# Reordering the mixer of an attention and RWKV/mLSTM network, and its first norms, on one core

## The chip, the cores and the metric

The kernel runs as one program on 1 core of one Trainium2 chip. The metric is the device time of one execution in microseconds. The core has five engines with instruction streams of their own: TensorE (PE, with weight loads as PEld), VectorE (DVE), ScalarE (ACT), GpSimd (POOL) and SyncE (SP, which here only issues DMAs). Each stream runs in order; semaphores tie them together.

## What the reference computes

Everything is float32, 256 tokens of width 1024. Two networks run one after the other.

The first has two layers over `x` (256 tokens) and a context `ctx` (256 tokens). In each layer both are normed and modulated, projected, and go through windowed attention and a Fourier mix, an output projection and a SwiGLU. The shifts and gains of the modulation come from `silu(c) @ w_ada`, a product of 1024 by 6144 for each layer (the "ada" chunks):

```
h  = rmsnorm(x,   g) * (1 + sc1)  + sh1
hc = rmsnorm(ctx, g) * (1 + csc1) + csh1
p = h @ w_in ; kv = hc @ w_in[:, kv]          # 10 column tiles of 128
```

The second has two layers: SwiGLU, mixer, SwiGLU. The mixer projects the normed tokens to 47 column tiles (r, k, v, low-rank inputs, mq, mk, mo, mv, gates) and runs two recurrences in chunks of 64 tokens. RWKV-7 needs for each head and chunk five masked 64x64 products of the scaled r, k, kk and b, and an inverse. mLSTM needs a causal convolution of mq and mk with four taps, a scan over its forget gates, and scores weighted by exponentials:

```
out = conv_b + sum_j w[j] * z[t - 3 + j]       # mq and mk, then silu
kk = k*k_k / ||k*k_k|| ; a = sigmoid(..) ; decay = exp(-exp(w_log))
S = S*w - (S kk) b^T + v k^T ;  y = S r        # done in chunks of 64
```

## The kernel before, in words

All features lie on partitions, tokens along the free axis. Weights come in chunks of 1 MB (two tiles of 128 columns) through `ring_a`, two slots; SP issues a load when the chunk before it in that slot has been used (`load_a`, line 478). In the second network each product is made of three products of rounded parts (`split_product`, lines 1645 to 1647): ACT rounds a weight tile to `t_hi` (`round_t`, L817), and DVE (tiles 0 to 16 of the mixer) or POOL (from tile 17, `rest_t`, L554) forms the rest `t_lo`. `t_hi` and `t_lo` hold two tiles, so tile t+2 is rounded only when tile t has been multiplied.

**The start.** Eight ada chunks come first: two in `ring_a`, six loaded ahead into `work` (L493). `ada` multiplies a chunk (L1592), ACT copies the row (L744), `ada_turn` turns it (L1603), DVE adds the bias (L1011). The norms of `x` and `ctx` follow ada chunks 5 and 6: squares on ACT (L596), their sums (L1615), two small products (L1624, L1633), then DVE scales by gain and norm (L1040) and ACT adds the shift (L767). Two more ada chunks (`B0`) stand between the norms and the first projection (L1717), which waits for all of it. Layer 0's attention takes 9 ada chunks in each of its two calls, one for each step over pairs of heads.

**The middle of the mixer**, in each of its two layers. TensorE's order: tiles 0 to 17, three low-rank products, tiles 18 to 26 (in layer 1 the value-residual product after tile 23), sums of squares for the head norms (L1964), their spread over the channels (L1972), the bonus sums (L1977), value tiles 27 and 28 (`value_tiles`, L1919), transposes of v (L1984), the two gate rows (L1994, L1995), transposes of khc and bhc, value tiles 29 and 30, and the unit products at, a, mrt, mt, art (`per_unit`, L2018). Then comes the front of the mLSTM heads (from L2062), which waits for DVE's last mask, for the silu of the convolution and for the gate rows.

DVE's order: shifts of tiles 0 to 14, the norm and decay chain (L1292 to L1340), the scaled operands kt, bh, kh, rt, khc, bhc (L1344 to L1352), all four taps of the convolution (L1362 and L1365, 32 instructions), the gate rows (L1374 to L1389), the masks of the unit products (L1393, L1410 to L1416). ACT empties tiles in order, between sigmoids, exponentials, the moves of the transposed tiles (L904) and the silu (L925).

Of the kernel before, what the change touches and what calls it, by code (L numbers as in the profile page):

```python
# [23 lines left out]
ALU = mybir.AluOpType  # L24
# [3 lines left out]
P = 128  # L28
# [27 lines left out]
ADA_STEP0, ADA_STEP1 = 9, 12  # L56
# [115 lines left out]
def program(nc, wa, wd, c1_in, c2_in, vec_in, small_in, four_in, x_in, ctx_in, out):  # L172
    with ExitStack() as ctx:
# [85 lines left out]
        def const1(name):  # L259
# [43 lines left out]
        in_loaded, vec_loaded, c2_loaded, const_loaded, small_loaded, out_stored = (  # L303
            sem(n) for n in ("in_loaded", "vec_loaded", "c2_loaded", "const_loaded", "small_loaded", "out_stored"))
# [30 lines left out]
                    "kt", "bh", "kh", "rt", "khc", "bhc", "at", "x1", "xt1", "x", "xt", "mrt", "mt", "art",  # L335
                    "s1", "ym", "yc", "yq", "s2", "yr", "yn", "gn", "gb", "ya"])
        RA = Steps(["tanh", "sgx", "sw", "aa", "gg", "rsq", "e0", "e1", "e2", "vt", "khct", "bhct", "ysd", "yT"])
        RP = Steps(["lw", "la", "lg", "ss", "rnb", "bon", "vt", "khct", "bhct", "at", "a", "mrt", "mt", "art", "yT"])
# [8 lines left out]
        MVS = Steps(["c0", "c1", "c2", "c3", "mn", "lf", "F", "g", "M", "fm", "nm", "hc"]  # L347
# [33 lines left out]
        ada_parts = [("0", ADA_FIRST - ADA_EARLY), ("early", ADA_EARLY), ("B0", ADA_FILL), ("L0", 2 * ADA_STEP0), ("M00", ADA_FILL), ("M01", ADA_FILL),  # L381
# [50 lines left out]
        def fill(name):  # L432
            return range(ada_from[name], ada_from[name] + ADA_FILL)
# [135 lines left out]
        def _(act):  # L569
            act.dma_start(vec[:, :], vec_in).then_inc(vec_loaded, 16)  # L570
            act.dma_start(c2[:, :], c2_in).then_inc(c2_loaded, 16)
            act.dma_start(x[:, :, :], x_in).then_inc(in_loaded, 16)
            act.dma_start(xc, ctx_in).then_inc(in_loaded, 16)
# [5 lines left out]
            def norm(key, src, call=None, ready=None, onto=None, first=None, also=None, summed=None):  # L579
# [26 lines left out]
                act.wait_ge(norm_sum, n + 1)  # L606
                nc.scalar.copy(nrt[:, :], ps[:, norm_bank(key), 0:T]).then_inc(norm_part, 1)
                act.wait_ge(norm_tok, n + 1)
# [138 lines left out]
            for g in range(ADA_FIRST):  # L747
                ada(g)
                if g == ADA_FIRST - 4:
                    act.wait_ge(in_loaded, 32)  # L750
                    act.wait_ge(c2_loaded, 16)
                    norm(("pre_mix", 0, 0), x[:, :, :])
                if g == ADA_FIRST - 3:
                    norm(("pre_mix", 0, 1), xc)
            act.dma_start(c1, c1_in).then_inc(const_loaded, 16)
            act.dma_start(wfour.rearrange("p a b -> p (a b)"), four_in).then_inc(const_loaded, 16)
            fcall = acall = 0
            for l in range(LAYERS):
# [4 lines left out]
                for which in range(2):  # L763
                    for k in range(KD):
                        act.wait_ge(norm_scaled, n_two[("pre_mix", l, which)] * KD + k + 1)
                        to = h2[:, k, token_cols(l, which)]
                        ins = nc.scalar.activation(to, to, ACT.Identity, bias=shift_of(l, 0, which)(k))  # L767
                    ins.then_inc(norm_out, 1)
                for g in fill(f"B{l}"):
                    ada(g)  # L770
                stage, n_q, n_blk = f"proj1{l}", (2 * T, T)[l], (4, 2)[l]
# [32 lines left out]
            for l in range(LAYERS):  # L804
# [31 lines left out]

                def empty_values(t):

                    act.wait_ge(t_done, l * NT2 + t + 2)
                    both = ps[:, 5 if t == MV else 7, :].rearrange("p (b s n) -> p s b n", b=2, s=2)  # L840
# [20 lines left out]
                empty_t(15)  # L861
# [5 lines left out]
                empty_t(16)  # L867
# [10 lines left out]
                empty_t(17)  # L878
                act.wait_ge(rw_p, RP.at("lg", l))
                nc.scalar.copy(gg, ps[:, 6:8, :].rearrange("p a (b t) -> p (a b) t", t=T)).then_inc(rw_a, 1)  # L880
                for t in range(18, 24):
                    empty_t(t)
# [6 lines left out]
                for t in range(24, MV):  # L889
                    empty_t(t)  # L890
# [1404 lines left out]
```

## Time and profile before

| | us |
|---|---|
| median of 3 runs | 2630.38 (2629.23 to 2631.09) |
| the profiled execution | 2632.37 |
| its span | 2630.5 |
| busy in the span: PE / PEld / DVE / ACT / POOL | 2446.0 / 2212.9 / 1257.7 / 995.0 / 220.3 |

The span runs from the first instruction to the last; 1.87 us of the execution lie around it. PE is busy for 93% of the span. That PE is busy does not say that it runs at full clock: the granted clock, 1.00 being 2.4 GHz and 0.50 being 1.2 GHz, is a column of its own where a table of stretches is shown.

### The profile page before, as it was taken

The numbers are of one execution on the slowest core, as the hardware profiler recorded it, in microseconds if no ns is written. First come the engines' busy times: TensorE is split into PE (matmuls) and PEld (weight loads), VectorE is DVE, ScalarE is ACT, GpSimd is POOL, SyncE is SP. The second block draws the span as 40 slices with busy tenths as digits, with TensorE's granted clock in tenths as the row PEclk, the third lists the DMA queues.
The fourth block names the chain that finished last, engine by engine and source line by source line (L and its number), as shares of the span: only waits on it lengthen the run. The fifth ranks groups of instructions, "written<-read, shape, count | busy, mean of one in ns | idle before, by whom it ended". The sixth has DMA issues, their size and how long they took to land.

```text
span 2630.5 us, 50338 instructions
## 1 busy us (share of the span) xinstructions
PE 2446.0 (93%) x20748; PEld 2212.9 (84%) x20748; DVE 1257.7 (48%) x2006; ACT 995.0 (38%) x1579; POOL 220.3 (8%) x199
## 2 busy tenths in 40 slices
PE   6989799989989889989999898999999997989998
PEld 3755499879966689989998788899999996888998
DVE  1043165455523255555564753455555548443554
ACT  2054343353333353343345332334434354321433
POOL 0000000000000000010004231100100032321000
PEclk9999899989989989999999799999999998999999
DMA  6144355345413455434433122554444341114552
GB/s 270 65 156 165 112 192 191 112 184 191 175 73 144 177 193 183 175 140 184 183 109 140 41 74 82 211 185 175 168 176 183 112 155 54 66 66 160 196 187 96
DMA packets 64487, 388.06 MB, mean 148 GB/s; under 512 B 7152, under 2 KB 7280, under 8 KB 27376
## 3 DMA queue, kind: packets, MB, share of 16 engines
q1 hardware_dynamic: 63216, 379.61, 39.6%
q10 hardware_dynamic: 864, 5.16, 0.5%
q8 instruction: 90, 1.47, 0.2%
q0 software_dynamic: 288, 1.57, 0.2%
q14 instruction: 29, 0.24, 0.0%
HBM read 385.27 MB, written 1.05 MB: 147 GB/s over the span
## 4 chain that ended last, share of the span: by engine, by line
PE 81%; DVE 9%; ACT 4%; DMA 3%; issue 2%; POOL 2%; SPq 0%; DVEq 0%; POOLq 0%; ACTq 0%
PE ps L1645 19%; PE ps L1646 19%; PE ps L1647 19%; PE ps L1717 5%; PE ps L1730 2%; PE ps L2150 2%; DMA ring_a<-in_wa 2%; PE ps L2018 2%; PE ps L2188 2%; POOL h_lo L532 1%; PE ps L1615 1%; PE ps L2123 1%; DVE nsq L1365 1%; PE ps L1592 1%; DVE work L1143 1%
## 5 line engine op out<-in xcount | busy, mean ns | idle before, releaser
L1645 PE MATMUL ps<-h_hi,w_hi 128*128 128x256 f32 x2464 | 701.9, 285 | 12.4 <-DVE mod L1011 8.7
L1646 PE MATMUL ps<-h_lo,w_hi 128*128 128x256 f32 x2464 | 699.9, 284 | 0.0
L1647 PE MATMUL ps<-h_hi,w_lo 128*128 128x256 f32 x2464 | 699.7, 284 | 0.0
L1645 PEld LDWEIGHTS ps<-h_hi,w_hi 128*128 128x128 f32 x2464 | 475.8, 193 | 14.6 <-DVE mod L1011 9.6
L1646 PEld LDWEIGHTS ps<-h_lo,w_hi 128*128 128x128 f32 x2464 | 475.9, 193 | 0.1
L1647 PEld LDWEIGHTS ps<-h_hi,w_lo 128*128 128x128 f32 x2464 | 475.7, 193 | 0.0
L1070 DVE TENSOR_TENSOR w_lo<-ring_a,w_hi 128x1024 fp32r<-128x1024 f32 x308 | 366.5, 1231 | 30.3 <-ACT w_hi L621 30.1
L1645 PE MATMUL ps<-hid_hi,d_hi 128*128 128x256 f32 x1232 | 348.7, 283 | 0.0
L1646 PE MATMUL ps<-hid_lo,d_hi 128*128 128x256 f32 x1232 | 348.7, 283 | 0.0
L1647 PE MATMUL ps<-hid_hi,d_lo 128*128 128x256 f32 x1232 | 348.6, 283 | 0.0
L621 ACT CAST w_hi<-ring_a 128x1024 fp32r<-128x1024 f32 x308 | 306.0, 1044 | 62.0 <-DMA ring_a<-in_wa 62.0
L1104 DVE TENSOR_TENSOR hid<-sg,ps 128x256 f32<-128x256 f32 x154 | 64.9, 421 | 550.9 <-ACT sg L652 550.8
L652 ACT ACTIVATE sg<-ps 128x256 f32<-128x256 f32 x154 | 59.1, 384 | 684.8 <-PE ps L1647 684.8
L1645 PEld LDWEIGHTS ps<-hid_hi,d_hi 128*128 128x128 f32 x1232 | 236.5, 192 | 0.0
L1646 PEld LDWEIGHTS ps<-hid_lo,d_hi 128*128 128x128 f32 x1232 | 236.5, 192 | 0.0
L1647 PEld LDWEIGHTS ps<-hid_hi,d_lo 128*128 128x128 f32 x1232 | 236.5, 192 | 0.0
L1645 PE MATMUL ps<-h_hi,t_hi 128*128 128x256 f32 x688 | 203.1, 295 | 7.9 <-POOL h_lo L532 3.8
L1077 DVE TENSOR_TENSOR d_lo<-ring_d,d_hi 128x1024 fp32r<-128x1024 f32 x154 | 190.3, 1236 | 19.7 <-ACT d_hi L629 16.7
L629 ACT CAST d_hi<-ring_d 128x1024 fp32r<-128x1024 f32 x154 | 161.6, 1049 | 98.3 <-PE ps L1647 98.3
L532 POOL TENSOR_TENSOR h_lo<-nsq,h_hi 128x256 fp32r<-128x256 f32 x72 | 60.8, 869 | 1647.0 <-ACT h_hi L640 922.0
L1646 PE MATMUL ps<-h_lo,t_hi 128*128 128x256 f32 x688 | 197.0, 286 | 0.0
L1647 PE MATMUL ps<-h_hi,t_lo 128*128 128x256 f32 x688 | 196.6, 286 | 0.0
(275 smaller groups left out, 3304.1 us busy)
## 6 DMA issues: line engine op xcount, KB each, us to landing
ring_a<-in_wa SPq DMA_DIRECT2D x278, 1024.0 KB, 4.8
ring_d<-in_wd SPq DMA_DIRECT2D x154, 512.0 KB, 5.3
work<-in_wa SPq DMA_DIRECT2D x6, 1024.0 KB, 22.0
work<-in_small POOLq DMA_DIRECT2D x2, 768.0 KB, 5.7
c<-in_c ACTq DMA_DIRECT2D x1, 1175.0 KB, 10.8
work<-in_c ACTq DMA_DIRECT2D x1, 1088.0 KB, 4.9
x<-in_x ACTq DMA_DIRECT2D x1, 1024.0 KB, 15.2
work<-in_ctx ACTq DMA_DIRECT2D x1, 1024.0 KB, 19.6
```

What stands on the lines that cost most here:

```text
L532: nc.gpsimd.tensor_tensor(h_lo[:, k, :], nsq[:, k, :], h_hi[:, k, :].bitcast(F32), ALU.subtract)\
L621: nc.scalar.copy(w_hi[:, f % 2, part], ring_a[:, c % 2, part]).then_inc(hi_a, 1)
L629: nc.scalar.copy(d_hi[:, f % 2], ring_d[:, d % 2]).then_inc(hi_d, 1)
L652: nc.scalar.activation(sg[:, f % 2, :], ps[:, 4 + f % 2, 0:T], ACT.Silu).then_inc(sg_ready, 1)
L1070: ins = nc.vector.tensor_tensor(w_lo[:, f % 2, part], ring_a[:, c % 2, part], w_hi[:, f % 2, part].bitcast(F32), ALU.subtract)
L1077: nc.vector.tensor_tensor(d_lo[:, f % 2], ring_d[:, d % 2], d_hi[:, f % 2].bitcast(F32), ALU.subtract)\
L1104: nc.vector.tensor_tensor(hid[:, f % 2, :], sg[:, f % 2, :], ps[:, 4 + f % 2, T:2 * T], ALU.mult)\
L1645: nc.tensor.matmul(out, hi, to_hi, start=start, stop=False, skip_group_check=True)
L1646: nc.tensor.matmul(out, hi, to_lo, start=False, stop=False, skip_group_check=True)
L1647: return nc.tensor.matmul(out, lo, to_hi, start=False, stop=stop, skip_group_check=True)
L1717: mm = nc.tensor.matmul(ps[:, 4 + p % 2, 0:cols.stop - cols.start], ring_a[:, slot, i % 2, k, :], h[:, k, cols], start=(k == 0), stop=(k = ...
L1730: mm = nc.tensor.matmul(ps[:, 4 + p % 2, b * P:(b + 1) * P], h[:, k, b * P:(b + 1) * P], ring_a[:, slot, i % 2, k, :], start=(k == 0), sto ...
```

## The change

Start: the norm of `x` and that of `ctx` are spread between ada chunks 3 to 7. For layer 0, `x` is scaled by its norm alone, before the gain is known, and ACT applies gain and shift together (`shifted`), alternating between `x` and `ctx` for each of the 8 channel tiles. The first projection tile waits for one channel tile of `ctx` at a time (`h2_part`) and no longer for the whole norm. `B0` is gone; its two chunks go to layer 0's attention, whose step 4 takes two chunks in each call. The DMAs of the constants are issued after the 16 shifts. In layer 1 ACT now copies the two B1 rows ahead of the 16 shifts, and DVE adds their bias halfway in the second norm.

Mixer: the head-norm sums stand behind tile 18, the spread and the bonus behind tile 21, then tile 22, the transposes of v, tile 23, products at and a, tile 24, transposes of khc, product mrt, tile 25, products art and mt, tile 26, transposes of bhc, value tiles 27 and 28, the gate rows, value tiles 29 and 30. DVE masks each product in between; the convolution follows the last mask. ACT writes the first tap of the convolution while it empties tiles 15 to 22 (`empty_conv`).

```diff
-("B0", ADA_FILL)
+("B0", 0)
-each = [1 if l == 0 or n % 4 else 2 for n in range(PAIRS + 1)]
+each = [2 if n % 4 == 0 and (l or n == 4) else 1 for n in range(PAIRS + 1)]
...
+            def shifted(which, k):
+                act.wait_ge(norm_scaled, n_two[("pre_mix", l, which)] * KD + k + 1)
+                gains = gain_of(l, 0, which)(k) if (l, which) == (0, 0) else 1.0
+                return nc.scalar.activation(to, to, ACT.Identity, scale=gains, bias=shift_of(l, 0, which)(k))
...
+            def empty_conv(t):
+                act.wait_ge(t_done, l * NT2 + t + 1)
+                k, src = t - MQ, ps[:, 4 + t % 2, 0:T]
+                nc.scalar.activation(z[:, t, 1:T + 1], src, ACT.Copy)
+                nc.scalar.activation(nsq[:, k, :], src, ACT.Identity, scale=vcol(f"tap3{l}", k),
+                                     bias=vcol(f"conv_b{l}", k)).then_inc(t_free, 1)
+                round_t(t + 2)
...
+                    if mixed is not None and k < KD - 1:
+                        pe.wait_ge(h2_part, mixed * (KD - 1) + k + 1)
...
             # TensorE, the mixer behind the low-rank products
+                tile(18)
                 # layer 1: value-residual product; head-norm sums (L1964 before)
+                for t in range(19, 22):
+                    tile(t)
                 # spread (L1972), bonus (L1977)
+                tile(22)
+                pe.wait_ge(rw_a, RA.at("gg", l))
+                to_tokens(z[:, V0:V0 + QT, 1:T + 1], 6).then_inc(rw_p, 1)
+                tile(23)
+                pe.wait_ge(rw_v, RV.at("bh", l))
+                per_unit(0, bh, kt).then_inc(rw_p, 1)
+                per_unit(2, kt, bh).then_inc(rw_p, 1)
+                tile(24)
+                pe.wait_ge(rw_v, RV.at("khc", l))
+                pe.wait_ge(rw_a, RA.at("vt", l))
+                to_tokens(khc, 6).then_inc(rw_p, 1)
+                pe.wait_ge(rw_v, RV.at("at", l))
+                per_unit(0, kh, rt).then_inc(rw_p, 1)
+                tile(25)
+                pe.wait_ge(rw_v, RV.at("x1", l))
+                per_unit(2, bh, rt).then_inc(rw_p, 1)
+                pe.wait_ge(rw_a, RA.at("khct", l))
+                per_unit(6, kh, kt).then_inc(rw_p, 1)
+                tile(26)
+                pe.wait_ge(rw_v, RV.at("mrt", l))
+                to_tokens(bhc, 0).then_inc(rw_p, 1)
+                value_tiles(MV)
+                pe.wait_ge(rw_v, RV.at("art", l))
                 # gate rows (L1994, L1995)
+                value_tiles(MV + 2)
```

## Rows read from the trace of the kernel before

**Rows 1.** The page: the chain that ended last, shares by engine.

```profile
PE 81%; DVE 9%; ACT 4%; DMA 3%; issue 2%; POOL 2%; SPq 0%; DVEq 0%; POOLq 0%; ACTq 0%
```

**Rows 2.** Chain of waits in the first 90 us: start, duration, what.

```profile
21.64 1.93 PE ps L1592 x16
...
46.69 0.19 DVE gain L1022
...
53.67 5.35 DMA ring_a<-in_wa
...
59.15 31.14 PE ps L1717 x67
```

**Rows 3.** Stretches: length, busy (instructions) by engine, granted clock, DMA share, GB/s.

```profile
21.64:51.60 29.96, 23.30 (x156) 13.57 (x160) 4.70 (x17) 11.94 (x28) 0.00 (x0) 1.00 0.62 252
1407.57:1434.77 27.20, 26.97 (x217) 26.16 (x216) 7.76 (x10) 11.57 (x17) 21.59 (x17) 1.00 0.44 155
1440.73:1448.00 7.27, 7.27 (x17) 5.34 (x17) 3.47 (x3) 2.95 (x3) 0.00 (x0) 0.50 0.00 0
1461.45:1468.92 7.47, 7.47 (x50) 7.34 (x52) 7.40 (x21) 5.25 (x9) 0.00 (x0) 0.77 0.21 89
1468.85:1474.66 5.81, 5.81 (x193) 5.68 (x192) 5.78 (x9) 3.82 (x5) 4.03 (x3) 1.00 0.03 6
1489.50:1503.90 14.40, 14.40 (x43) 11.85 (x44) 2.23 (x4) 2.13 (x4) 0.00 (x0) 0.50 0.00 0
```

**Rows 4.** Timeline of ACT, first products: start, busy, line, what, idle before.

```profile
47.41 3.30 ACT L767 ACTIVATE work<-work,mod 128x256 f32<-128x256 f32 x8 [2.32 <-DVE work L1040]
68.44 0.37 ACT L775 COPY work<-ps 128x256 f32<-128x256 f32 x1 [12.47 <-PE ps L1717]
```

**Rows 5.** Timeline of PE, three steps of layer 1's attention.

```profile
840.86 1.13 PE L1771 MATMUL ps<-work 64*128 64x512 f32 x4 [0.20 <-ACT work L700]
...
846.37 1.13 PE L1771 MATMUL ps<-work 64*128 64x512 f32 x4 [0.52 <-ACT work L700]
...
853.79 1.13 PE L1771 MATMUL ps<-work 64*128 64x512 f32 x4
```

**Rows 6.** Layer 1's first projection: chain of waits.

```profile
759.13 4.91 DMA ring_a<-in_wa
```

**Rows 7.** Timeline of PE: spread, transposes, value tiles and front, both mixers.

```profile
1440.73 3.77 PE L1972 MATMUL ps<-work,c 8*128 8x256 f32 x8 [4.06 <-DVE work L1332]
...
1456.34 1.97 PE L1984 MATMUL ps<-c,work 128*128 128x128 f32 x16
...
1461.45 0.35 PE L1919 MATMUL ps<-t_hi,h_hi 128*128 128x256 f32 x1 [3.15 <-POOL t_lo L554]
...
1489.50 3.75 PE L2062 MATMUL ps<-work,c 4*128 4x256 f32 x8 [4.70 <-DVE work L1393]
...
2182.25 3.77 PE L1972 MATMUL ps<-work,c 8*128 8x256 f32 x8 [5.84 <-DVE work L1332]
...
2230.96 3.75 PE L2062 MATMUL ps<-work,c 4*128 4x256 f32 x8 [5.26 <-DVE work L1393]
```

**Rows 8.** Timeline of DVE in both mixers.

```profile
1437.91 0.98 DVE L1330 TENSOR_SCALAR work<-work 8x256 f32<-8x256 f32 x1 [22.52 <-ACT work L892]
...
1440.60 1.15 DVE L1334 TENSOR_TENSOR work<-work 128x1024 f32<-128x1024 f32 x1
...
2166.20 1.49 DVE L1308 TENSOR_TENSOR work<-vfirst,work 128x1024 f32<-128x1024 f32 x1 [22.62 <-ACT work L886]
...
2170.34 5.02 DVE L1318 TENSOR_SCALAR work<-work,vec,omka 128x256 f32<-128x256 f32 x4
```

**Rows 9.** Timeline of POOL between the value tiles, mixer layer 0.

```profile
1456.20 5.10 POOL L554 TENSOR_TENSOR t_lo<-ring_a,t_hi 128x512 fp32r<-128x512 f32 x4 [17.45 <-ACT t_hi L817]
```

**Rows 10.** Timeline of ACT between the value tiles and the front.

```profile
1455.07 2.00 ACT L817 CAST t_hi<-ring_a 128x1024 fp32r<-128x1024 f32 x2
...
1476.66 1.91 ACT L925 ACTIVATE nsq<-nsq 128x2048 f32<-128x2048 f32 x1 [3.87 <-DVE nsq L1365]
```

More of the change, by code:

```diff
@@ L55 @@
 ADA_FILL = 2
-ADA_STEP0, ADA_STEP1 = 9, 12
+ADA_STEP0, ADA_STEP1 = 10, 12
 PAIRS = 8
@@ L605, in norm, with norm_squares, norm_rows, norm_root @@
                     also()
-                act.wait_ge(norm_sum, n + 1)
+                norm_rows(key)
+                norm_root(key)
+            def norm_squares(src):
+                for i in range(PIECES):
+                    k = slice(i * KD // PIECES, (i + 1) * KD // PIECES)
+                    nc.scalar.activation(nsq[:, k, :], src[:, k, :], ACT.Square).then_inc(norm_sq, 1)
+            def norm_rows(key):
+                act.wait_ge(norm_sum, n_id[key] + 1)
                 nc.scalar.copy(nrt[:, :], ps[:, norm_bank(key), 0:T]).then_inc(norm_part, 1)
+            def norm_root(key):
+                n = n_id[key]
                 act.wait_ge(norm_tok, n + 1)
@@ L744, in ada @@
                 nc.scalar.copy(ada_rows[:, u, :], ps[:, 4 + u, 0:T]).then_inc(ada_row, 1)
[L747 to L756, printed above, removed]
+            first, second = ("pre_mix", 0, 0), ("pre_mix", 0, 1)
+            ada(0)
+            ada(1)
+            ada(2)
+            act.wait_ge(c2_loaded, 16)
+            act.wait_ge(x_loaded, 16)
+            nc.scalar.activation(warm[:, 0:1], const("one"), ACT.Sqrt)
+            norm_squares(x[:, :, :])
+            ada(3)
+            norm_rows(first)
+            act.wait_ge(xc_loaded, 16)
+            norm_squares(xc)
+            ada(4)
+            norm_root(first)
+            ada(5)
+            norm_rows(second)
+            ada(6)
+            norm_root(second)
+            ada(7)
             fcall = acall = 0
@@ L1026, in gains, with inverse, norm @@
                 dve.wait_ge(gain_ready, done)
-            def norm(key, src, gains, dst, shifted=False, onto=None, also=None):
+            def inverse(key):
+                dve.wait_ge(norm_rt, n_id[key] + 1)
+                nc.vector.reciprocal(nst[:, 2:4], nst[:, 0:2]).then_inc(norm_rstd, 1)
+            def norm(key, src, gains, dst, shifted=False, onto=None, halfway=None):
                 n = n_id[key]
@@ L1032, in norm @@
                     dve.wait_ge(norm_scaled, n_two[key] * KD)
-                dve.wait_ge(norm_rt, n + 1)
-                nc.vector.reciprocal(nst[:, 2:4], nst[:, 0:2]).then_inc(norm_rstd, 1)
-                if also is not None:
-                    also()
+                inverse(key)
                 dve.wait_ge(norm_all, n + 1)
@@ L1057, in norm @@
                 for k in range(KD):
+                    if k == KD // 2 and halfway is not None:
+                        halfway()
                     ins = scale(k)
@@ L1948, in _ @@
                 mm.then_inc(rw_p, 1)
-                for t in range(18, 24):
-                    tile(t)
+                tile(18)
                 if l:
@@ L1956, in _ @@
                     mm.then_inc(vres_p, 1)
-                for t in range(24, MV):
-                    tile(t)
                 pe.wait_ge(rw_v, RV.at("kq", l))
@@ L1966, in _ @@
                 mm.then_inc(rw_p, 1)
+                for t in range(19, 22):
+                    tile(t)
                 pe.wait_ge(rw_v, RV.at("rn", l))
```

239 lines of the change are left out of this document (125 added, 114 removed).

## The prediction

> **What bounds the kernel now.** I read the page's chain first. It lies on TensorE for 81% and on DVE for 9% [rows 1], so work of other engines matters only where TensorE stands still or runs slowly for it. Then I read the chain and the timelines where the change is. There are two kinds of such places.
>
> At the start the first projection begins at 59.15 although its inputs are nearly ready: its weights are asked for at 53.67, when the first B0 chunk has freed the slot, and take 5.35 us [rows 2]. Before that, from 21.64 to 51.60, TensorE is busy for 23.30 of 29.96 us [rows 3].
>
> In each mixer there are two stretches. First DVE stands for 22.52 us (layer 0) and 22.62 us (layer 1) and waits for ACT, which waits for products that TensorE issues behind its tiles [rows 8]. Then TensorE in turn waits for DVE, and the spread starts at 1440.73 and 2182.25 behind 4.06 and 5.84 us of idle time, the front at 1489.50 and 2230.96 behind 4.70 and 5.26 us [rows 7]. From spread to front it is 48.8 and 48.7 us. The clock falls there: 0.50 from 1440.73 to 1448.00 and 0.50 over the 14.4 us from the front on [rows 3], which is 1.2 GHz where the tiles ran at 2.4 GHz (1.00 from 1407.57 to 1434.77).
>
> **The start.** In the new order TensorE issues, from 21.64 on, the same kinds and numbers of instructions as it did up to 51.60: five ada chunks (3 to 7) with their turns, two sums, two pairs of token products, two spreads. Their busy time is 23.30 [rows 3], so with some 0.9 us of short waits it is through at 45.8. The last bias and the gain follow, as before at 46.69 [rows 2]; I take 46.4. Now `x` needs only ACT for each channel tile. ACT's 16 shifts take 3.30/8 = 0.41 each [rows 4], the second one waits one DVE scaling (about as long), so TensorE's first product can start at 47.4 and the last of the 8 channel tiles is there at 46.5 + 16 x 0.41 = 53.1. The weights are no wait any more: with B0 gone, SP asks for them as soon as ada chunks 0 and 1 are used, before 15 us, and those loads stand behind the early chunks exactly as the B0 loads did. Before, tile 0 took from 59.15 to 68.44, 9.3 us [rows 2, 4]. Now it ends between 54.0 (ACT bound) and 47.4 + 9.3 = 56.7 (as slow as it was). I take 55.0, since the idle time in front shrinks from 1.5 us behind other pauses to 1.6 us behind dense work: **-13.4 us** (-11.7 to -14.4). The constants' DMAs move from before the shifts to behind them, 0.8 us of issue on ACT while tile 0 runs; their first reader comes six tiles later, so nothing.
>
> **The two chunks that moved.** They go into step 4 of each attention call of layer 0. Layer 1 has such steps already: a step with one chunk lasts 846.37 - 840.86 = 5.5, one with two 853.79 - 846.37 = 7.4 [rows 5]. The lower price is 1.9; against the 5.1 us of an undisturbed step it would be 2.3. I take 2.3 for the first call and 2.7 for the second, whose steps are shorter while each chunk still needs about 5 us to land [rows 6]: **+5.0 us** (+3.8 to +7).
>
> **Layer 1's first norms.** ACT's 16 shifts now come behind the copies of both B1 rows, so they start near 760.7 and not at 755.4. The first product needs the 8 of `x` and one of `ctx`: 760.7 + 9 x 0.41 = 764.4. Before it waited for a load from 759.13 to 764.04 [rows 6], which the change leaves. **0** (-1 to +2).
>
> **The mixers, up to the spread.** One tile costs 27.20/9 = 3.02 [rows 3]. In layer 0 the head-norm sums (about 1.9, half of what the like spread took at the low clock [rows 7]) follow tile 18, and tiles 19 to 21 stand before the spread: 1407.6 + 2.9 + 1.9 + 3 x 3.02 = 1421.4 instead of 1440.73, so **-19.3**. DVE is ready by then: its chain ended at 1437.91 - 22.52 = 1415.4 [rows 8], the inverse root and its reciprocal need about 3 us more.
> In layer 1 (its times are layer 0's plus 737.1) the value-residual product also stands behind tile 18, and DVE's wait for it ends at about 1414.3 instead of 1429.1. From there to the spread DVE needed 2182.25 - 2166.20 = 16.0 [rows 7, 8], which gives 1430.3 instead of 1445.1, **-14.8**. TensorE then idles some 6 us before the spread, more than the 5.84 of before, so I give the spread and the bonus their old 7.5 us at 1.2 GHz, whereas in layer 0 they come behind dense tiles and take 3.8.
>
> **From spread to front.** At full clock, TensorE's order adds up to: spread and bonus 3.8, five tiles (22 to 26) 14.4, at 7.47 x 0.77 / 2 = 2.88 without waits, since a value pair is two tiles' work [rows 3], three sets of transposes at 1.0 (1.97 for two [rows 7]) 3.0, five unit products at 5.81/3 = 1.94 [rows 3] 9.7, and 1.1 for the wait on the second mask in layer 0: 32.0. Behind tile 26 the serial part begins, and it is the main cost of the change:
> - tile 28 can be rounded only when tile 26 is done and emptied: 0.4 + 1.04 on ACT, 2.5 to 3 on POOL (5.10/4 for each half [rows 9]), less the 1.0 of the transposes: 3.6;
> - value tiles 27 and 28: their like, 29 and 30, took 7.47 at a mean clock of 0.77 behind 3.15 us of idle time [rows 3, 7], and I take that;
> - tiles 29 and 30 can be rounded only now: emptying 0.65, one t_hi 1.0 [rows 10], four halves on POOL 5.1 [rows 9], together 6.9. Before, three sets of transposes and the gate rows stood in this gap and all but 3 us of it was used; now only the gate rows (1.0) do, and 5.9 is idle;
> - value tiles 29 and 30: 7.47;
> - ACT empties them 0.65, rounds two more tiles 2.0, loads a table 1.28 and makes the silu 1.91 [rows 10], which the front waits for: 6.1 with the gaps between. Before, DVE's convolution was later than this and hid it; now the convolution is through before value tiles 29 and 30.
> Sum 63.5 where it was 48.8. Layer 0: -19.3 + 14.7 = **-4.6**. Layer 1: no wait of 1.1, but 3.7 more for spread and bonus at the low clock, 66.1 against 48.7: -14.8 + 17.4 = **+2.6**. Together **-2.0**.
> The bounds: all value tiles at 2.4 GHz save 1.7 x 4 = 6.8; all of them wholly at 1.2 GHz (7.47 x 0.77 / 0.50 = 11.5 each) cost 16.1 more. The front itself ran at 0.50 for 14.4 us [rows 3]; the idle time in front of it grows from 4.7 to 6.1, so I leave it as it is.
>
> **What hides the rest.** The first tap on ACT adds 0.28 for each of 8 tiles, where ACT waits for TensorE anyway; it takes eight instructions off DVE. The masks read PSUM and lie between the tiles.
> DVE and POOL hinder each other: four scalings of 128x256 lasted 5.02 us in layer 1 [rows 8], where POOL was making t_lo, against 1.15 for a whole 128x1024 product without it. The 16.0 us that I use hold this already. The Trainium skill, "SBUF — State Buffer", section "Who interferes with whom", says that a VectorE instruction with two SBUF inputs and a GpSimd instruction that reads SBUF exclude each other for the whole instruction. That speaks against this change, since POOL's rests of tiles 22 to 28 now fall among DVE's unit work. It is my rival C.
> For the clock: the Trainium skill, "TensorE: Matmul & The Clock Gate", section "Why this matters for your kernels", says that idle gaps between bursts bring the array back to half its clock. By it the new gaps of 5.9 and 6.1 us cost what I have taken or more; without it rival A holds.
>
> **The sum.** -13.4 + 5.0 + 0 - 2.0 = -10.4. The profiled execution took 2632.37, its span 2630.5. From it the forecast is 2622.0; it lies 2.0 above the median of 2630.38, so for a median I say **2620.0**.
>
> **The rivals.**
> - A, the clock stays up. Value tiles at full clock (-6.8) and spread and bonus of layer 1 too (-3.7): 2620.0 - 10.5 = 2609.5. For it: more of TensorE's idle time is filled than before. Against it: value tiles behind only 3.15 us of idle time had 0.77. Chance 0.15.
> - B, the mixers give back more. Each value pair loses twice as much to the clock as the one in the rows, 1.7 x 4 = 6.9: 2626.9, no change that can be told. For it: the gaps of 5.9 us are longer than the 3.15. Against it: that pair was back at full clock before its end, since the unit products behind it had 1.00 [rows 3]. Chance 0.15.
> - C, the other side: POOL's halves queue behind DVE's long instructions. For tiles 22 to 28 each of two halves waits up to 1.15 for one, 2.3 a tile; seven tiles in two mixers make 32.2, if none of it has slack: 2652. For it: DVE works without pause from the spread to the last mask. Against it: a unit product or transposes stand between most tiles, 2 to 4 us of slack. Slower by 0.2% needs 15.6 us of it, about half. Chance 0.08.
> - D, the start gives less: should ACT's shifts and the pauses take the place of the load, with tile 0 ending at 60, it is 2625.0. Chance 0.07.
>
> **How the numbers follow.** The forecast has 0.55, with its own range of 2614 to 2626. 0.2% is 5.3 us, about what a measurement of this kernel can tell from no change: faster means below 2625.1, slower above 2635.6. Faster: A 0.15, most of the forecast 0.51, half of D 0.04, together 0.70. Slower: most of C and the tail of B, 0.09. Same: 0.21. The range leaves out the far half of C and of A: 2608 to 2632.
>
> **What would show it.** Right: the first projection at 47 to 48 and its tile 0 out by 57; two steps of layer 0's attention at about 7.4; the spreads some 19 and 15 us earlier against their mixer's start; 60 to 68 us from spread to front, with TensorE idle before both value pairs and before the front, the last one ended by ACT's silu. Wrong: DVE, not ACT, ending the wait at the front; TensorE waiting for t_lo before tiles 22 to 26 for more than 1 us each; a clock of 1.00 in the value tiles; a wait for weights at the first projection.

## The result, and the profile after

The changed kernel takes 2617.99 us (median of 5, 2613.37 to 2618.90); the kernel before, beside it, 2630.14 (5 runs, 2627.39 to 2631.09). The ratio is 0.9942, 95% interval 0.9932 to 0.9953. The forecast was 2620.0. The profiled execution took 2617.78, its span 2615.8: 14.7 us less than the span of before, which belonged to an execution 2.2 above its median.

The chain of the changed kernel by engine, against [rows 1]:

```profile
PE 79%; DVE 5%; issue 5%; POOL 4%; ACT 4%; DMA 2%; POOLq 0%; SPq 0%; DVEq 0%; ACTq 0%
```

TensorE has lost 2 points and DVE 4; POOL has gained 2 and issue (time in which an engine waited for nothing that the profile shows) 3.

**The start**, TensorE's timeline of the changed kernel (start, busy, line, what, idle before), against [rows 2, 3]. L1654 is an ada chunk, L1677 the sums, L1783 the projection:

```profile
24.11 1.93 PE L1677 MATMUL ps<-nsq,c 128*32 128x256 f32 x16
25.82 1.93 PE L1654 MATMUL ps<-work,cs 128*32 128x256 f32 x16
...
28.99 1.07 PE L1654 MATMUL ps<-work,cs 128*32 128x256 f32 x16
...
31.08 1.07 PE L1677 MATMUL ps<-nsq,c 128*32 128x256 f32 x16
...
36.41 0.51 PE L1665 MATMUL ps<-c,ada_rows 128*128 128x2 f32 x4
38.53 11.80 PE L1783 MATMUL ps<-work,ring_a 128*128 128x512 f32 x23 [1.62 <-ACT work L792]
```

From 28 on an ada chunk takes 1.07 us and not 1.93. The same instruction on the same data is 1.8 times as fast, so TensorE is at its higher clock there. In the profile of before all of them, up to 55, took 1.93 or close to it, while the column of the granted clock said 1.00 [rows 3]. In these profiles that column does not tell the speed at the start, before its first change; the duration of a known instruction does. Tile 0 leaves TensorE at 47.37, where it was 68.44. Its first products are slow again, in two stretches up to its end:

```profile
38.50:42.00 3.50, 3.47 (x5) 1.44 (x6) 2.08 (x6) 3.50 (x9) 0.00 (x0) 0.52 0.18 32
42.00:47.40 5.40, 5.40 (x14) 2.49 (x13) 0.00 (x0) 2.65 (x7) 0.00 (x0) 0.99 0.72 287
```

**Layer 0's attention**, the same timeline: a step of 5.1 us, then the one with two chunks, 7.43:

```profile
141.28 1.13 PE L1837 MATMUL ps<-work 64*128 64x512 f32 x4 [0.40 <-ACT work L713]
...
146.40 1.13 PE L1837 MATMUL ps<-work 64*128 64x512 f32 x4
...
153.83 1.13 PE L1837 MATMUL ps<-work 64*128 64x512 f32 x4
```

**The mixers**, TensorE's timeline of the changed kernel, against [rows 7]. L2040 is the spread, L1988 the value pairs, L2133 the front:

```profile
1404.90 0.36 PE L1707 MATMUL ps<-h_hi,t_hi 128*128 128x256 f32 x1 [1.25 <-POOL t_lo L555]
1407.94 1.99 PE L2040 MATMUL ps<-work,c 8*128 8x256 f32 x8
1442.57 0.55 PE L1988 MATMUL ps<-t_hi,h_hi 128*128 128x256 f32 x1 [3.37 <-POOL t_lo L555]
...
1457.87 0.55 PE L1988 MATMUL ps<-t_hi,h_hi 128*128 128x256 f32 x1 [5.81 <-POOL t_lo L555]
...
1471.55 3.75 PE L2133 MATMUL ps<-work,c 4*128 4x256 f32 x8 [5.89 <-ACT nsq L977]
...
2150.71 3.77 PE L2040 MATMUL ps<-work,c 8*128 8x256 f32 x8 [7.12 <-DVE work L1397]
```

Stretches of the changed kernel (columns as in [rows 3]): the two value pairs and the front of layer 0, then the two value pairs of layer 1:

```profile
1442.57:1451.10 8.53, 8.53 (x49) 8.40 (x50) 5.73 (x15) 0.00 (x0) 0.00 (x0) 0.66 0.00 0
1457.87:1465.66 7.79, 7.79 (x48) 7.59 (x48) 2.66 (x6) 0.00 (x0) 0.00 (x0) 0.73 0.22 93
1471.55:1485.95 14.40, 14.40 (x43) 11.85 (x44) 2.23 (x4) 3.34 (x5) 0.75 (x1) 0.50 0.15 64
2189.02:2196.52 7.50, 7.50 (x49) 7.37 (x50) 5.74 (x15) 0.00 (x0) 0.00 (x0) 0.77 0.01 2
2203.28:2210.51 7.23, 7.22 (x48) 7.02 (x48) 2.67 (x6) 0.00 (x0) 0.00 (x0) 0.80 0.23 95
```

**Where the time went, by stage.** DVE makes one small reciprocal for each norm. Its start marks the stages well, because the same instruction stands at the same place in every kernel. The table has these starts from the profiled execution of each run (us): the norm of `ctx` at the start, the norm behind layer 0's output projection, the last of layer 1's first norms; the lengths of the two mixers, from their norm to the norm behind them; and the last norm.

| kernel | ctx norm | out, layer 0 | layer 1 | mixer 0 | mixer 1 | last |
|---|---|---|---|---|---|---|
| before | 50.2 | 303.9 | 755.6 | 340.9 | 346.5 | 2622.0 |
| changed | 35.6 | 287.8 | 740.6 | 338.2 | 349.7 | 2607.3 |
| start_only | 35.2 | 286.3 | 740.7 | 341.3 | 346.3 | 2606.4 |
| mixer_only | 47.1 | 302.3 | 755.7 | 337.6 | 349.8 | 2621.2 |
| b0_only | 47.1 | 302.0 | 755.8 | 343.2 | 346.3 | 2624.6 |
| whole_norm | 39.6 | 297.3 | 750.6 | 340.2 | 350.1 | 2623.1 |
| silu_first | 35.8 | 288.2 | 742.5 | 331.9 | 343.7 | 2594.6 |
| gap_fill | 35.7 | 288.1 | 741.3 | 331.6 | 343.7 | 2593.8 |
| hi_first | 35.4 | 287.8 | 740.8 | 326.0 | 336.7 | 2583.1 |
| dve_rest | 39.5 | 288.8 | 742.6 | 326.4 | 342.8 | 2591.2 |
| early_root | 35.4 | 287.8 | 741.5 | 333.7 | 337.5 | 2590.3 |
| start_fill | 36.1 | 285.7 | 738.9 | 331.0 | 343.1 | 2591.2 |
| best | 39.6 | 292.5 | 745.6 | 320.6 | 328.4 | 2576.0 |
| wide_first | 39.9 | 297.2 | 750.6 | 319.0 | 326.9 | 2575.7 |

Changed against before: 15.0 us are won by layer 1's first norms, and the mixers add -2.7 and +3.2.

The same program differs between executions. The mixer of `before` and `b0_only` is the same code, 340.9 and 343.2. Single cells are good to about 2 us, and more at the start (below).

### The profile page after: what moved, and what is told of

The parts are those of the page before. It is cut to its first block, busy times and chain, and to the rows that moved or that the text cites. A ratio compares the mean times of both kernels' runs of the same rounds, so it can differ in the third digit from the quotient of the medians.

```text
span 2615.8 us, 50326 instructions
## 1 busy us (share of the span) xinstructions
PE 2434.9 (93%) x20748; PEld 2207.6 (84%) x20748; DVE 1248.7 (48%) x1990; ACT 1002.4 (38%) x1594; POOL 224.7 (9%) x199
## 4 chain that ended last, share of the span: by engine, by line
PE 79%; DVE 5%; issue 5%; POOL 4%; ACT 4%; DMA 2%; POOLq 0%; SPq 0%; DVEq 0%; ACTq 0%
PE ps L1707 19%; PE ps L1708 19%; PE ps L1709 19%; PE ps L1783 5%; POOL t_lo L555 3%; PE ps L1796 2%; PE ps L2221 2%; PE ps L2068 2%; DMA ring_a<-in_wa 2%; POOL h_lo L533 1%; PE ps L2259 1%; PE ps L1677 1%; PE ps L2194 1%; PE ps L1654 1%; PE ps L1811 1%
## 5 line engine op out<-in xcount | busy, mean ns | idle before, releaser
L1707 PEld LDWEIGHTS ps<-h_hi,w_hi 128*128 128x128 f32 x2464 | 476.6, 193 | 14.7 <-DVE mod L1063 9.6
## 6 DMA issues: line engine op xcount, KB each, us to landing
c<-in_c ACTq DMA_DIRECT2D x1, 1175.0 KB, 10.4
x<-in_x ACTq DMA_DIRECT2D x1, 1024.0 KB, 14.8
work<-in_ctx ACTq DMA_DIRECT2D x1, 1024.0 KB, 19.3
```

Source lines behind the costliest of these rows:

```text
L1707: nc.tensor.matmul(out, hi, to_hi, start=start, stop=False, skip_group_check=True)
```

## The experiments

### One part alone

`start_only` has the new start and first norms and the old mixers, `mixer_only` the reverse.

> The kernel before with the changed start, B0 chunks and layer 1 norms only; the mixers are the old ones. Theory 1 (the mixers cancel, -3.0 and +2.9 in the two profiles): all of the gain is here, 0.994 of the kernel before (2615 to 2619), first projection near 38.5 and its tile 0 out near 47.4, spread to front 48.8 as before. Rival (the new mixer has a hidden part in the gain, for instance through the 1.9 us that were lost between the attention and the second network): 0.996 to 0.997, 2620 to 2623.

> The kernel before with the new mixers only. Theory 1: within 0.1% of the kernel before (2630 +-2); layer 0 about 3 us shorter and layer 1 about 3 us longer, 63.6 and 65.7 us from spread to front. Rival: 4 us faster or more, 2626 or less.

Measured: `start_only` 2616.75 against 2632.73, ratio 0.9945 (0.9932 to 0.9959). `mixer_only` 2635.41, ratio 1.0010 (1.0001 to 1.0019), its mixers 3.3 us shorter and 3.3 longer. All of the gain is in the new start and first norms; the rivals of both are out. The new mixers as they stand are worth nothing, if not slightly less.

`b0_only` moves the two chunks and nothing else:

```diff
-("B0", ADA_FILL)
+("B0", 0)
-each = [1 if l == 0 or n % 4 else 2 for n in range(PAIRS + 1)]
+each = [2 if n % 4 == 0 and (l or n == 4) else 1 for n in range(PAIRS + 1)]
```

> The kernel before with only the two B0 chunks moved to step 4 of layer 0's two attention calls; the order of the norms stays. Theory 1: the weights of the first projection are there early, but the shifts of ctx end at 55.4, so the first product moves from 59.15 to 55.6 (-3.6); the two longer steps give back 4.2 to 5; the small products of the start stay at 1.93 us an ada chunk. Together +1, 2631, no change that can be told. Rival (the late load of the weights was most of the start's gain, and the order of the norms adds little): the start is 8 us or more shorter and the time 2626 or less.

Measured: 2634.90, ratio 1.0010 (1.0001 to 1.0019), as theory 1 had it. The first product came at 52.49 and not at 55.6, because this execution had its fast stretch early, as `mixer_only` had. TensorE's timeline of `mixer_only`, whose start is the old code:

```profile
41.19 1.07 PE L1601 MATMUL ps<-work,cs 128*32 128x256 f32 x16
...
55.73 2.68 PE L1726 MATMUL ps<-work,ring_a 128*128 128x512 f32 x3 [2.01 <-DMA ring_a<-in_wa]
```

The like rows of before are an ada chunk of 1.93 at 42.72 and the first product at 59.15. So the same code differs by 3.4 us between two executions. That difference does not last: 3.1 us at the norm of `ctx` (50.2 and 47.1) are 1.6 at the norm behind the output projection and nothing at the next norm (318.02 in before, 318.08 in `mixer_only`). Against `mixer_only` the moved chunks give 3.2 us at the start (55.73 to 52.49) and all but 0.3 of it is gone at the norm behind the output projection (302.3 and 302.0): the two longer steps cost 2.9 us.

### The wait by channel tiles

`whole_norm` is the changed kernel with the old wait at the first projections:

```diff
-                        project(stage, i, h2, slice(0, 2 * T), mixed=l)
+                        project(stage, i, h2, slice(0, 2 * T))
...
+                pe.wait_ge(norm_out, n_id[("pre_mix", l, 1)] + 1)
```

> The changed kernel, but its first projections wait for the whole norm of ctx, as before the change, and no longer for one channel tile at a time. Theory 1 (the wait by channel tiles is worth two things: it overlaps tile 0 with the shifts, and it leaves TensorE no 8 us of idle time that would halve its clock): the last shift ends at 44.6, the first product starts near 44.9 and tile 0 takes about 9.4 us at half clock, out near 54.5 where it was 47.37: 2618 + 7 = 2625. Rival (the clock does not depend on that pause): tile 0 takes 4.8 us and is out near 49.7: 2620.

Measured: 2631.09 (11 runs, 2624.81 to 2642.65), ratio 0.9999 (0.9987 to 1.0011): the whole gain is gone, 13 us by the medians where the expected time has 7. TensorE's and ACT's timelines:

```profile
33.53 1.94 PE L1677 MATMUL ps<-nsq,c 128*32 128x256 f32 x16
...
37.92 1.07 PE L1654 MATMUL ps<-work,cs 128*32 128x256 f32 x16
...
49.30 1.19 PE L1783 MATMUL ps<-work,ring_a 128*128 128x512 f32 x1 [7.79 <-issue]
```

```profile
58.67 0.37 ACT L815 COPY work<-ps 128x256 f32<-128x256 f32 x1 [9.47 <-PE ps L1783]
```

At its own place theory 1 holds: the first product has the double duration of 1.19 behind 7.8 us of idle time, and tile 0 takes 9.4 us. From the first shift to tile 0 it is 58.67 - 41.95 = 16.7 us against 47.37 - 37.36 = 10.0 in the changed kernel: 6.7 us for the wait. One thing was missing in it: in layer 1 the same wait costs 3.0: from its first norms (750.6 and 740.6 in the table) to the norm behind its output projection (910.4 and 897.4) it is 159.8 against 156.8 us. The shifts start 4.6 us later than in the changed kernel because the small products of this execution sped up at 37 and not at 28. The edit stands behind those products, and `dve_rest`, `best` and `wide_first`, which have no such edit, sped up as late in their profiles; so this belongs to the execution. The two waits make 9.7 us; why the medians differ by another 3.4 no run settles.

### The pauses in the mixer

`silu_first` is the changed kernel with two steps of ACT exchanged:

```diff
-                empty_values(MV + 2)
                 act.wait_ge(ml_v, MVS.at("c3", l))
                 nc.scalar.activation(nsq[:, :, :], nsq[:, :, :], ACT.Silu).then_inc(ml_a, 1)
+                empty_values(MV + 2)
```

> The changed kernel, ACT makes the convolution's silu before it empties value tiles 29 and 30 and rounds tiles 31 and 32, not behind them. Theory 1 (the 5.9 us of idle time in front of the front are ACT's order and nothing else): DVE's convolution is through at 1448, the silu ends near 1459.5, before the value tiles end at 1465.7; the front starts some 0.9 us behind them, 5 us earlier in each mixer: 2618 - 10 = 2608. If the clock then stays at 2.4 GHz over the front (14.4 us at 1.2 GHz now), up to 4 us more for each: 2600. Rival (DVE's gate rows or POOL's t_lo of tiles 31 and 32 are as late, the front's own tiles then wait for what the front no longer waits for): 2 us or less, 2616 to 2618.

Measured: 2608.47 against 2632.73, ratio 0.9917 (0.9903 to 0.9930), which is 6.6 us better than the changed kernel by the ratios. TensorE's timeline:

```profile
1466.11 1.96 PE L2133 MATMUL ps<-work,c 4*128 4x256 f32 x8 [0.83 <-ACT work L892]
```

The pause of 5.89 is 0.83, and the first products of the front take 1.96 and not 3.75. The mixers are 6.3 and 6.0 us shorter. The pause was ACT's order. By the medians the gain is 9.5 us; the profiled execution was the fastest of its five. The clock did not stay up: from 1468.8 to 1479.0 the granted clock is 0.52.

The next four start from `silu_first`. `hi_first` changes the order within a value pair (the comment stands for the loop's lines):

```diff
+                    pe.wait_ge(t_hi_ready, p0 + t + 2)
                     for b in range(2):
+                        # t_hi products of the block, then (b = 0: wait for t_lo) its t_lo products
```

> The last kernel (silu first), and in each value pair TensorE makes the 16 products of the first block of tokens with t_hi before it waits for t_lo; the other 32 follow. Theory 1 (what TensorE waits for ahead of the value pairs is POOL's t_lo, 3.37 and 5.81 us of idle time, and it is this idle time that brings the clock down in them): the pairs start when t_hi is rounded, some 2 and 4 us earlier, and end 2 to 3 us earlier each, more where the clock then stays at 2.4 GHz; the front starts 4 to 9 us earlier in each mixer: 2608 - 8 to - 16 = 2592 to 2600. Rival (the clock falls in any case and the 16 products run at half speed, 3.4 us instead of 1.9, so that only the wait is filled with slower work): the front starts 2 us earlier or less in each, 2605 or more.

Measured: 2593.47 against 2632.46, ratio 0.9848 (0.9835 to 0.9862). TensorE's timeline, the starts behind a wait:

```profile
1439.52 0.36 PE L1991 MATMUL ps<-t_hi,h_hi 128*128 128x256 f32 x1 [0.62 <-ACT t_hi L857]
1442.31 1.18 PE L1991 MATMUL ps<-t_lo,h_hi 128*128 128x256 f32 x8 [0.65 <-POOL t_lo L555]
1449.09 0.36 PE L1991 MATMUL ps<-t_hi,h_hi 128*128 128x256 f32 x1 [1.76 <-ACT t_hi L857]
1453.20 1.19 PE L1991 MATMUL ps<-t_lo,h_hi 128*128 128x256 f32 x8 [1.96 <-POOL t_lo L555]
1459.59 0.67 PE L2137 MATMUL ps<-work,c 4*128 4x256 f32 x2 [0.83 <-ACT work L892]
```

The pause of 3.37 is now 0.62 and 0.65, the one of 5.81 is 1.76 and 1.96. The mixers are 5.9 and 7.0 us shorter, within theory 1.

`dve_rest` gives `t_lo` of tiles 29 and 30 to DVE (POOL's loops, which leave them out, are not shown):

```diff
+                rest_t(MV + 2)
+                rest_t(MV + 3)
                 def m(name):
```

> Silu first, and DVE makes t_lo of value tiles 29 and 30 behind the convolution, where POOL made it (128x512: DVE 0.65 us, POOL 1.25). Theory 1: DVE is idle by then, the wait ahead of the second value pair falls from 5.81 to about 3 us, and the pair itself may lose less to the clock: 3 to 5 us in each mixer, 2608 - 6 to - 10 = 2598 to 2602. Rival (DVE is not free: its convolution ends at 1448, or the gate rows then come later than the front needs them): 2 us or less, 2606 to 2609.

Measured: 2596.48, ratio 0.9862 (0.9847 to 0.9877). DVE's four halves and the pair behind them:

```profile
1451.68 2.50 DVE L1337 TENSOR_TENSOR t_lo<-ring_a,t_hi 128x512 fp32r<-128x512 f32 x4 [1.87 <-ACT t_hi L860]
```

```profile
1454.33 0.35 PE L1994 MATMUL ps<-t_hi,h_hi 128*128 128x256 f32 x1 [3.35 <-DVE t_lo L1337]
```

2.50 us where POOL takes 4.92; the wait is 3.35. The profile has 5.5 us in layer 0, where both value pairs ran at full clock, and 0.9 in layer 1, where they did not. A part of the 5.5 is not the edit's: the first value pair of layer 0, ahead of it, took 5.9 us behind the same 3.37 us of idle time behind which it took 8.5 in the changed kernel. So a pause of that length brings the clock down in one execution and not in another. The median lies beyond theory 1's range, 1.5 us below it, and the profile is of the slowest execution, 5.1 above the median; what the others gained inside was not seen.

`early_root` moves DVE's inverse norm ahead of the bonus's four scalings:

```diff
-"kp", "rkr", "rnmax", "rn", "l0"
+"kp", "rnmax", "rn", "rkr", "l0"
...
+                if l:            # behind the spread, before the bonus
+                    tile(22)
```

> Silu first, and DVE makes the inverse norm before the four scalings of the bonus, not behind them; in layer 1 tile 22 stands between spread and bonus. Theory 1 (the 7.1 us of idle time ahead of layer 1's spread are DVE's order: the four scalings take 5.59 us beside POOL, 2.71 in layer 0 without it): the spread of layer 1 moves from 2145.8 to about 2140.5, runs at 2.4 GHz (1.99 and not 3.77), and the unit products come 5 to 8 us earlier; layer 0 does not change. 2608 - 5 to - 8 = 2600 to 2603. Rival (DVE's whole chain up to kt and bh bounds layer 1, not the spread): the products come 2 us earlier or less, 2606 or more.

Measured: 2604.03, ratio 0.9892 (0.9877 to 0.9907), mixer 1 6.2 us shorter. TensorE's timeline in layer 1, the spread and the first unit product, then a tile of layer 0:

```profile
2141.40 1.99 PE L2040 MATMUL ps<-work,c 8*128 8x256 f32 x8 [2.57 <-DVE work L1393]
...
2154.49 1.72 PE L2071 MATMUL ps<-work 64*64 64x64 f32 x51 [1.07 <-DVE work L1410]
```

```profile
1407.34 0.36 PE L1707 MATMUL ps<-h_hi,t_hi 128*128 128x256 f32 x1 [2.48 <-POOL t_lo L555]
```

The spread stands behind 2.57 us and not 7.12, the unit products start at 2154.49 and not 2160.43. The median misses theory 1's 2600 to 2603 by 1 us. Layer 0 did not stay as it was: that mixer is 1.8 us longer, because POOL's `t_lo` is later there. One half of it, begun while DVE makes the four scalings, took 3.32 us, where four take 4.92 ahead of the second value pair. POOL's timeline:

```profile
1403.87 3.32 POOL L555 TENSOR_TENSOR t_lo<-ring_a,t_hi 128x512 fp32r<-128x512 f32 x1 [2.36 <-ACT t_hi L857]
```

`start_fill` puts 8 products of the identity behind ada chunks 1 and 2.

> Silu first, and 8 transposes of the identity, whose result nobody reads, behind ada chunk 1 and again behind ada chunk 2, in the pauses of 1.86 and 2.02 us in which TensorE waits for weights. Theory 1 (the first products run at half speed because TensorE had paused, and speed up at 28 because it no longer does): ada chunks 3 and 4 take 1.07 us where they took 1.93, the first projection starts 1.5 to 3 us before 38.66, and the time is 2605 to 2607. Rival (the speed follows something else, such as time since the start or the DMAs): the same instructions change speed at the same time as before, within 0.5 us, and 2608 stays.

Measured: 2604.29, ratio 0.9899 (0.9886 to 0.9913), whose interval overlaps with that of `silu_first`. TensorE's timeline:

```profile
18.30 1.50 PE L1654 MATMUL ps<-work,cs 128*32 128x256 f32 x16
...
22.16 1.07 PE L1654 MATMUL ps<-work,cs 128*32 128x256 f32 x16
...
30.27 1.94 PE L1677 MATMUL ps<-nsq,c 128*32 128x256 f32 x16
...
38.98 6.23 PE L1783 MATMUL ps<-work,ring_a 128*128 128x512 f32 x10 [1.61 <-ACT work L792]
```

With the pauses filled the speed is up from 19. In the ten other profiles with the new start it comes up between 27 and 38, so this one profile speaks for theory 1's cause. The first projection gains nothing by it (38.98 for 38.66): a chunk's load still ends a wait of 1.21 us ahead of 27.82, and the speed is lost again at 30. The expected 1.5 to 3 us there were a miss. The profile is 3.6 us ahead by layer 1's first norms, but not where the edit is, so the lower median is not put down to the edit.

### The clock by itself

`gap_fill` is the changed kernel with products that nobody reads in the pauses ahead of the value pairs and the front. The first wait for a mask moves ahead of the first of them:

```diff
+                pe.wait_ge(rw_v, RV.at("art", l))
+                spend(12)
                 value_tiles(MV)
...
+                spend(20)
                 value_tiles(MV + 2)
+                spend(20)
```

> The changed kernel with products of the identity, whose result nobody reads, in its three pauses behind tile 26 in each mixer: 12 ahead of the first value pair (3.37 us idle now), 20 ahead of the second (5.81) and 20 ahead of the front (5.89). They take some 0.235 us each at 2.4 GHz, so the waits end when they did. Theory 1 (idle time costs twice, once as a wait and once as a halved clock behind it): the value pairs take 5.9 us where they took 7.2 to 8.5, the front's first 8 us run at 2.4 GHz and take 4 to 5, together 6 to 9 us in each mixer: 2618 - 12 to - 18 = 2600 to 2606. Rival (the front is slow because its products are narrow, 4 rows, and the clock falls under them in any case): only the value pairs gain, 1.5 to 2.6 us each: 2609 to 2613.

Measured: 2608.61 against 2632.32, ratio 0.9916 (0.9901 to 0.9931). Stretches of layer 0: value pairs and front.

```profile
1441.56:1447.55 5.99, 5.99 (x49) 5.86 (x50) 5.74 (x15) 0.00 (x0) 0.00 (x0) 1.00 0.00 0
1454.35:1460.33 5.98, 5.98 (x50) 5.98 (x51) 2.66 (x6) 0.00 (x0) 0.00 (x0) 1.00 0.29 121
1466.23:1480.35 14.12, 14.12 (x57) 12.12 (x58) 2.23 (x4) 3.33 (x5) 0.76 (x1) 0.64 0.17 71
```

Each theory is right for one part. The value pairs take 5.99 and 5.98 us at 2.4 GHz where they took 8.53 and 7.79 behind the same time between the products: its being idle cost them 4.4 us more in layer 0. The two pairs of layer 1 are at 1.00 too; without the filling the first pair of layer 0 was in the profiles of `dve_rest` and `mixer_only`, and no pair in that of the changed kernel. The front starts at full speed and still falls to half within 2.5 us, with no pause in it and products before it up to 1.43 us ahead. The median lies between the two forecasts. In the profile the mixers are 6.5 and 6.0 us shorter, by the medians it is 9.4 us together.

### The parts together

`best` is `silu_first`, `hi_first` and `dve_rest` together, and `early_root` in layer 1 alone.

> Silu first, products with t_hi first, DVE's t_lo of tiles 29 and 30, and the inverse norm ahead of the bonus in layer 1 alone (in layer 0 it made DVE wait and cost 1.9 us in one profile). Theory 1: the savings add up as far as they remove different waits. From the first with silu alone (2608): products first -15, of which DVE's t_lo removes the rest of the second pair's wait, about 1.9 in layer 0 and 0.5 in layer 1, and the inverse norm -6 in layer 1: 2593 - 2 - 6 = 2585. Rival (DVE's two t_lo tiles push the gate rows, which now bound the front): 2588 to 2592.

Measured: 2584.09 against 2632.32, ratio 0.9814 (0.9801 to 0.9828), as theory 1 had it. The savings do not simply add: the three medians lie 15.0, 12.0 and 4.4 us below that of `silu_first`, together 31.4, and `best` lies 24.4 below it. `hi_first` and `dve_rest` shorten partly the same wait, as the expectation says.

`wide_first` adds one exchange:

```diff
-                    if h < 3:
+                    if 0 < h < 3:
                         front(h + 1)
...
                     tile(gates_at("head", h)[0])
+                    if h == 0:
+                        front(1)
```

> The fastest kernel so far (2584), with gate tile 31 ahead of the second head's front products and no longer behind them. In all kernels the clock falls some 2 us after the front starts and is back about 10 us later, inside tile 31, also where TensorE was busy up to 0.8 us before. Theory 1 (the narrow products of the front, 4 rows, bring the clock down, and dense 128-row products bring it back): with tile 31 earlier the clock is back earlier, and each mixer gains 1 to 3 us: 2579 to 2582. Rival (the fall comes from the pauses before the front and lasts its time whatever stands in it): the time at half clock stays 10 us, 2583 to 2586.

Measured: 2576.13 (5 runs, 2574.08 to 2586.07) against 2632.23, ratio 0.9783 (0.9769 to 0.9796). The first two heads' front products and tile 31 of layer 0, from the first of them to the product behind them, in `best` and then in `wide_first`:

```profile
1461.13:1475.06 13.93, 13.93 (x56) 12.02 (x57) 2.23 (x4) 5.15 (x7) 4.94 (x4) 0.63 0.22 75
```

```profile
1465.31:1477.63 12.32, 12.32 (x57) 10.85 (x58) 1.67 (x3) 4.69 (x7) 4.93 (x4) 0.72 0.25 85
```

The same work takes 1.6 us less, at a granted clock of 0.72 and not 0.63. From these figures I estimate the time at half clock: twice (1 - 0.63) x 13.93 = 10.3 us in `best`, twice (1 - 0.72) x 12.32 = 6.9 us in `wide_first`. So the rival, by which it stays 10 us, is out, and theory 1, that the clock comes back earlier under the 128-row products, agrees. The mixers are 1.6 and 1.5 us shorter in this profile, 3.2 together. The median is 8.0 below `best` and 3 us below theory 1's range; that much is not explained. The profile is of the slowest of the five executions; the other four had a mean clock of 0.971 to 0.973 against 0.967 here, and their times are 8 to 12 us below it; what they look like inside was not seen.

## Why the prediction was right, point by point

- **The sum** was -10.4 against -14.7 between the profiles and -12.15 between the medians. The direction, the place of the gain and the total are right. In part that is luck: the start gave 7.7 us more than I had, the mixers gave back 0.5 where I had a gain of 2.0, and the profile of before, from which I summed, is of an execution 2.2 us above its median.
- **The start, -13.4, measured -21.1.** The step that failed is that the small products of the new order keep "their busy time 23.30". They took 15.29 us, since from 28 on they ran at twice the speed. I had read 1.00 in the granted clock as full speed and never compared 1.93 with the 1.07 that ada chunks take elsewhere. A part of the miss lies in the profile I read: 3.4 us of its start were that execution's own, as `mixer_only` shows. The shifts were slower than I took, 16 in 7.3 us (0.45 each, not 0.41). Tile 0 took 8.8 us where I had 7.6 (55.0 - 47.4), and it was not the shifts that bound it: they end at 44.6, and ACT then waits 2.75 us for TensorE, which worked without a pause, up to 42 at half its clock (0.52 in the stretch above). ACT's timeline:

```profile
47.37 0.37 ACT L815 COPY work<-ps 128x256 f32<-128x256 f32 x1 [2.75 <-PE ps L1783]
```

- **The wait by channel tiles** got no term of its own. `whole_norm` prices it at 6.7 us at the start and 3.0 in layer 1, and at 13 by the medians; without it nothing that can be told is left.
- **The two moved chunks, +5.0.** In the profile +0.6 and +3.6 (from the first call to the second 60.65 to 61.26, from there to the output projection 47.20 to 50.78), in `b0_only` 2.9 in all. The first call's step of two chunks is 7.43, as forecast. Another 2.1 us went behind the output projection, up to the second norm behind it, where the small products came at the low clock. That is not the change's doing: from the norm behind the output projection to the next it is 14.2 us in before and 15.4 in the changed kernel, but 15.8 in `mixer_only`, whose code is the old one there. TensorE's timeline of the kernel before and then of the changed one, sums and two ada chunks:

```profile
300.29 2.09 PE L1615 MATMUL ps<-nsq,c 128*32 128x256 f32 x16 [2.80 <-ACT nsq L596]
...
304.73 1.93 PE L1592 MATMUL ps<-ring_a,cs 128*32 128x256 f32 x32
```

```profile
283.40 2.53 PE L1677 MATMUL ps<-nsq,c 128*32 128x256 f32 x16 [2.80 <-ACT nsq L597]
...
289.19 2.91 PE L1654 MATMUL ps<-ring_a,cs 128*32 128x256 f32 x32
```

- **Layer 1's first norms, 0.** 0.8 us better (-15.0 to -15.8, at the norm behind layer 1's output projection), less than single profiles can tell.
- **The mixers.** Up to the spread -19.3 and -14.8 were forecast, -17.6 and -13.7 measured; 1.25 us of the first difference is a wait for POOL's `t_lo` ahead of tile 21. From spread to front 63.5 and 66.1 were forecast, 63.6 and 65.7 measured. The pauses of 5.9 and 6.1 are 5.81 and 5.89, the value pairs 7.2 to 8.5 where I had taken 7.47. The pause ahead of the first pair is 3.37; I wrote 3.6, though its terms as I give them add up to 2.9 to 3.4. Sum -4.6 and +2.6, measured -2.7 and +3.2: the spreads came 1.7 and 1.1 us later than I had them.
- **The signs I named** came but for two: the spreads 2 and 1 us off, TensorE idle ahead of both value pairs and the front, the last ended by ACT's silu, no wait for weights at the first projection. The first product, forecast at 47 to 48, came at 38.5; and only the first attention call has a step of 7.4, in the second the step with two chunks takes 6.1.
- **Rival A** (the clock stays up) did not happen; `gap_fill` shows that the clock does stay up in the value pairs once the pauses are filled, and does not in the front. **B** is out: against the 5.98 us of full clock the pairs lost 1.2 to 2.6 each, not 3.4. **C**, POOL behind DVE's long instructions, did not come about: ahead of tiles 22 to 26, where I had it, TensorE waits for `t_lo` in neither mixer. There are waits of 1.25 and 0.46 us ahead of tile 21, nothing near 15.6. **D** is out: tile 0 ended at 47.37.

The Trainium skill, "SBUF — State Buffer", section "Who interferes with whom", calls the port pair of VectorE and GpSimd an exclusive lock. The trace agrees: four scalings of 128x256 in DVE's timeline, in `silu_first` in layer 0, where POOL begins 1.0 us after the first of them, and in layer 1, where POOL works all the while.

```profile
1396.33 2.71 DVE L1391 SCALAR_TENSOR_TENSOR work<-work,vec 128x256 f32<-128x256 f32 x4
```

```profile
2138.18 5.59 DVE L1391 SCALAR_TENSOR_TENSOR work<-work,vec 128x256 f32<-128x256 f32 x4
```

A scaling takes 0.48 us while POOL is idle. In layer 1 each takes 1.4 to 1.5 us, as long as the POOL instruction beside it (1.44), three times its own time. The 2.71 us of layer 0, which I took in an expectation for the time without POOL, hold one such wait. In `early_root` it is the other way round: in layer 0 the four scalings take 1.56 us and POOL's half the 3.32 shown above. In layer 1 of the changed kernel this, together with DVE's order, put 7.12 us ahead of the spread; with the scalings moved behind, 2.57 are left.

"TensorE: Matmul & The Clock Gate", section "What's actually happening", of the Trainium skill says that the number of products at the low clock varies between runs of one kernel. The first products at 55.73 and 59.15, of the same code in two profiles, agree. For a drop of the clock in the middle of a kernel the same page of the Trainium skill, section "Why this matters for your kernels", names idle gaps; in the front of `gap_fill` the clock falls without one.

## What to carry to other kernels

Price a moved stretch of small products at both clocks: compare an instruction's duration with its like elsewhere in the trace before you call the clock full. When a wait is filled, what ends the next one is mostly an order written down for the old place; here exchanging two ACT steps, splitting a wait into the part that is ready and the rest, giving two tiles to an idle engine and moving two DVE instructions brought 34 us, nearly three times what the large change did. Take differences of less than 4 us at a start from several executions, or from medians, not from two profiles; and look whether such a difference is still there further on.

## What the runs showed of the hardware that was not expected

- The granted clock column read 1.00 over 29.96 us in which the same instructions took 1.93 us that take 1.07 elsewhere.
- TensorE's clock fell under products of 4 rows with no pause between them (0.64 over 14.12 us, idle time before it 1.43 us, `gap_fill`); with a tile of 128-row products moved up to stand between them the same work had 0.72 where it had 0.63 (`wide_first` and `best`).
- One and the same pause of 3.37 us ahead of the first value pair of layer 0 was followed by 8.53 us at a clock of 0.66 in the changed kernel and by 5.92 us at 1.00 in `dve_rest`.
- DVE and POOL instructions with operands in SBUF waited for one another by whole instructions: a scaling of 0.48 us took 1.4 to 1.5 beside POOL, and a POOL half of 1.23 took 3.32 beside DVE's scalings.
- The same start has two forms, 3 to 4 us apart: in the table the norm of `ctx` is at 35.2 to 36.1 or at 39.5 to 39.9 in the new order, and at 47.1 or 50.2 in the old.
